# Two seven-product groups in the first strip pair of each chunk of the second MLP's down-projection

## What is computed

```python
def causal_dwconv(u, conv_w, conv_b):
    ...
    for t in range(CONV_WIDTH):
        out = out + up[:, t:t + S] * conv_w[t]
...
        h = rms_norm_2(x, pre_ffn_g[l])
        up = causal_dwconv(h @ w_up[l], conv_w[l], conv_b[l])
        y = (jax.nn.gelu(up[..., :D_FF_2], approximate=True) * up[..., D_FF_2:]) @ w_down[l]
        x = x + rms_norm_2(y, post_ffn_g[l])
```

## Time and profile before

| | us |
|---|---|
| device time, median of 3 runs (2079.47 to 2080.83) | 2079.84 |
| the profiled execution's own time | 2080.22 |
| its span, first to last instruction | 2078.4 |
| TensorE busy | 2067.9 (99%) |
| VectorE busy | 1413.8 (68%) |
| ScalarE busy | 1136.4 (55%) |

### The profile page before, as it was taken

How to read it: one execution, slowest core, us unless ns; L and a number is a source line. 1 busy time by engine, 2 the same in 40 slices (tenths; PEclk the granted TensorE clock), 3 DMA queues, 4 the chain that set the end, 5 groups by cost and what they waited for, 6 DMA issues and landing times.

```text
span 2078.4 us, 24128 instructions
## 1 busy us (share of the span) xinstructions
PE 2067.9 (99%) x9229; PEld 1714.6 (82%) x9229; DVE 1413.8 (68%) x1618; ACT 1136.4 (55%) x1384; POOL 60.1 (3%) x55
## 2 busy tenths in 40 slices
PE   9999999999999999999999999999999999999998
PEld 7888888888888888888888888888888888888887
DVE  6446556777886779777876655566767775576665
ACT  7555655555554555555655544455555544555553
POOL 3000000000000000000002000000000000000010
PEclk9999999999999999999999999999999999999999
DMA  8687666778666776678678787677787757778763
GB/s 294 194 262 228 190 186 217 245 242 254 216 199 200 242 239 201 213 237 269 223 258 238 218 250 231 192 212 223 243 253 233 234 181 214 237 228 262 244 212 122
DMA packets 291907, 469.50 MB, mean 226 GB/s; under 512 B 18512, under 2 KB 82128, under 8 KB 291280
## 3 DMA queue, kind: packets, MB, share of 16 engines
q1 hardware_dynamic: 290928, 463.46, 71.5%
q10 hardware_dynamic: 864, 4.49, 0.6%
HBM read 432.75 MB, written 35.13 MB: 225 GB/s over the span
## 4 chain that ended last, share of the span: by engine, by line
PE 96%; DMA 2%; DVE 1%; ACT 1%; issue 0%; SPq 0%; ACTq 0%; DVEq 0%
PE ps L1842 96%; DMA passed_rows<-xN 1%; DVE Wl L1428 1%; DMA E<-passed_rows 0%; ACT Wh L1192 0%; DMA raw<-in_sb_w_qkv_dram 0%; DVE xN L1577 0%; DVE T L1587 0%; PE ps L1845 0%; SPq L1105 0%; ACT aHL L1214 0%; ACT T L1208 0%; DVE hid L1616 0%; DVE aHL L1591 0%; SPq L1100 0%
## 5 line engine op out<-in xcount | busy, mean ns | idle before, releaser
L1428 DVE TENSOR_TENSOR Wl<-raw,Wh 128x1024 fp32r<-128x1024 f32 x743 | 908.1, 1241 | 534.5 <-ACT Wh L1192 527.4
L1842 PE MATMUL ps<-Wh,aHL 128*128 128x512 f32 x3642 | 1129.2, 390 | 2.6 <-DVE aHL L1591 0.9
L1192 ACT ACTIVATE Wh<-raw 128x1024 fp32r<-128x1024 f32 x743 | 771.0, 1055 | 517.2 <-PE ps L1842 492.8
L1842 PEld LDWEIGHTS ps<-Wh,aHL 128*128 128x128 f32 x3642 | 684.0, 188 | 146.5 <-issue 1.7
L1842 PE MATMUL ps<-Wl,aHL 128*128 128x512 f32 x1821 | 708.7, 389 | 0.0
L1842 PE MATMUL ps<-Wh,hid 128*128 128x512 f32 x1548 | 480.2, 389 | 0.0
L1842 PEld LDWEIGHTS ps<-Wl,aHL 128*128 128x128 f32 x1821 | 342.1, 188 | 70.2
L1842 PEld LDWEIGHTS ps<-Wh,hid 128*128 128x128 f32 x1548 | 290.6, 188 | 60.5 <-DVE xN L1577 0.2
L1842 PE MATMUL ps<-Wl,hid 128*128 128x512 f32 x774 | 301.1, 389 | 0.0
L1842 PEld LDWEIGHTS ps<-Wl,hid 128*128 128x128 f32 x774 | 145.3, 188 | 30.0
L1842 PE MATMUL ps<-Wh,oHL 128*128 128x512 f32 x512 | 158.8, 390 | 0.0
(11 more groups left out here) (218 smaller groups left out, 1003.8 us busy)
## 6 DMA issues: line engine op xcount, KB each, us to landing
raw<-in_mlp_w_dram SPq DMA_DIRECT2D x256, 512.0 KB, 4.9
raw<-in_w_up_dram SPq DMA_DIRECT2D x176, 512.0 KB, 4.4
raw<-in_sb_w_qkv_dram SPq DMA_DIRECT2D x93, 512.0 KB, 5.1
raw<-in_w_down_dram SPq DMA_DIRECT2D x88, 512.0 KB, 4.7
raw<-in_w_in_dram SPq DMA_DIRECT2D x64, 512.0 KB, 5.2
passed_strip<-T SPq DMA_DIRECT2D x88, 256.0 KB, 4.4
T<-passed_strip SPq DMA_DIRECT2D x176, 128.0 KB, 4.5
raw<-in_sb_w_o_dram SPq DMA_DIRECT2D x32, 512.0 KB, 5.4
```

The costliest lines, as they stand in the source:

```text
L1192: e.activation(Wh[:, i % NW, c], src, ACT.Copy).then_inc(st["hi"][0], 1)
L1428: e.tensor_tensor(Wl[:, i % NW, c], src, Wh[:, i % NW, c].bitcast(F32), ALU.subtract).then_inc(st["lo"][0], 1)
L1842: return e.matmul(o, l, r, start=start, stop=stop, skip_group_check=True)
```

## The change

In the first strip pair of each chunk, the first two row pieces of both strips (`sevens=(2 * at, 2 * at + 1)`) become two groups. `lead` is new: 2n - 4 plain pieces of the first strip (8 in chunk 0, 6 in chunk 1), all but its tail, stand ahead of the first group; three pieces of the second strip stand between the groups, five (chunk 0) or three (chunk 1) behind the second, then the tails. Chunk 1 now makes mixed tokens for its first strip. In chunk 1 the fold adds to rows that exist (eight VectorE operations), and the steps `y_sum` wait for it. The diff, cut to its core:

```diff
@@ def strip_pair
-    def strip_pair(w, s4, ks, tail, mov, tiles, evacs, koff=0, sevens=(), fold=None):
+    def strip_pair(w, s4, ks, tail, mov, tiles, evacs, koff=0, sevens=(), fold=None, lead=None):
...
-        lead, gap = (4, 3) if tail else (2, 3 if len(plain) > 7 else 2)
+        lead, gap = (lead or 4, 3) if tail else (2, 3 if len(plain) > 7 else 2)
@@ def evac_conv
-    def evac_conv(j, which, t0, last, at_first):
+    def evac_conv(j, which, t0, last):
...
-                    if at_first and t0 in MIXED_STRIPS:
+                    if t0 in MIXED_STRIPS and (j < 6 or t0 == 0):
                         free["E"] = [lo, mix_tokens("hid2", "E", *MIXED_STRIPS[t0], [g])]
@@ def evac_y
-                kw = dict(t=t, s4=s4, set=s, mm=k[t], t0_free=list(free["T0"]), y=y, q=q, g=g, g_row=st["g_row"])
+                kw = dict(t=t, s4=s4, set=s, mm=k[t], t0_free=list(free["T0"]), y=y, q=q, g=g, g_row=st["g_row"],
+                          folded=st.get(("fold", s4)))
@@ the loop over the two chunks
             i = strip_pair("w_down_2", s4, tuple(range(2 * at, 2 * (at + n))), 0 if s4 else 2, "hid2", hid_tiles,
                            [evac_y(c, s4), evac_y(c, s4 + 1)], koff=2 * at,
-                           sevens=(2 * at, 2 * at + 1, 2 * at + 4) if c == 0 and s4 else (),
-                           fold=fold_into("xn", s4, fresh=True))
+                           sevens=(2 * at, 2 * at + 1, 2 * at + 4) if c == 0 and s4 else (2 * at, 2 * at + 1) if s4 == 0 else (),
+                           fold=fold_into("xn", s4, fresh=c == 0), lead=None if s4 else 2 * n - 4)
@@ vector_program, the steps y_sum and y_last
                     e.wait_ge(*st["mm"])
+                    if st["folded"]:
+                        e.wait_ge(*st["folded"])
                     e.tensor_tensor(xn[:, t, cs], xn[:, t, cs], ps[st["set"]][:, t, :], ALU.add).then_inc(st["y"][0], 1)
```

More of the change, by code:

```diff
@@ L798, in plan_program @@
             for which in range(2):
-                i = strip("w_up_2", which * 5632 + (at + j) * STRIP, ALL8, "aHL", tile_hl, evac_conv(at + j, which, 4 * j, j == n - 1, c == 0))
+                i = strip("w_up_2", which * 5632 + (at + j) * STRIP, ALL8, "aHL", tile_hl, evac_conv(at + j, which, 4 * j, j == n - 1))
                 if at + j + which == 0:
```

## The result

The changed kernel takes **2085.95 us** (median of 9 runs, 2082.85 to 2087.44) where the kernel before takes 2080.62 beside it (2079.47 to 2083.07): 1.0025 times as long, with an interval of 1.0016 to 1.0033. The forecast was 2081.9 with a range to 2084.0, so the time lies outside, on the slow side.

The account below looks back on a forecast made before the run. TensorE, busy 99%, was taken as the bound, so only removed matmuls could gain. Two pairs, each 2.28 + 0.10 - 1.36 = 1.02 us lost, add 2.0 to the median 2079.84: forecast 2081.9 us, range 2078.2 to 2084.0.

Parts of the forecast that it names:

- The matmuls: Two groups in each of two pairs remove 12 matmuls of 0.227 us: 2.72 us saved, 1.36 per pair.
- The wait: At the first plain piece behind either pair's second group, TensorE waits 2.28 us on `Wl`; bounds 1.1 to 3.4.
- X: The moment TensorE ends s1 (second split buffer) of the first group, releasing the split of a later plain piece.
- The chain: ScalarE's and VectorE's queued work from X until TensorE can start the plain piece behind the second group: 17.24 us.
- The other side of the sum: TensorE's work from X until the plain piece behind the second group is due: 66 matmuls, 14.96 us.
- the released split: ScalarE's split, starting at X, of the third plain piece between the groups; 1.09 us until VectorE's low half starts.
- the slow first matmul: The first matmul after a wait takes 0.33 us instead of 0.227, so 0.10 us was added per wait.
- What costs nothing: Mixed tokens, loads and later `y_sum` cost nothing; chunk 1's fold just fits, 9.38 us against 9.44.
- the rival that the clock falls in the gaps: Behind the new waits the clock drops to 1.2 GHz, one piece at either place, giving 2087.3 us; chance 0.05.
- the sum said 2.0: Both pairs together lose 2.0 us: per pair 2.28 + 0.10 - 1.36 = 1.02.
- The row leaned on: The stretch behind the 2.26 us gap shows a granted clock of 1.00, taken as no drop near that length.
- The gap leaned on: TensorE's 2.26 us gap before the last two matmuls, about the longest in the trace, compared with the expected 2.2 us.

Follow-up runs that it names:

- orders without a wait: Changed kernel with all plain pieces of the second strip between the groups (2077.88 against 2080.28; again 2078.15 against 2080.92), or five (2077.74 against 2080.92).
- the first series: The changed kernel's first timing against the kernel before: 2085.95 us against 2080.62, ratio 1.0025.
- the second series: The changed kernel timed once more, unaltered, against the kernel before: 2084.46 us against 2080.78, ratio 1.0018.

## Why the prediction was right and wrong

**The matmuls.** Right: 12 fewer, worth 2.7 us. The orders without a wait show it (2.4, 2.8 and 3.2 us below before), and in their profiles a pair is 1.33 to 1.36 us shorter.

**The wait.** Right in place and cause, and 0.27 us too small at either place. ScalarE's and VectorE's timelines of the changed kernel, chunk 1, from X on (the moment from which the prediction followed the queues; ScalarE starts there at 1986.36, in chunk 0 at 1642.73):

```profile
1986.36 1.06 ACT L1193 ACTIVATE Wh<-raw 128x1024 fp32r<-128x1024 f32 x1 [0.30 <-PE ps L1845]
...
1994.67 2.08 ACT L1349 ACTIVATE E<-T,conv 128x256 f32<-128x256 f32 x4 [2.49 <-DVE T L1552]
1996.66 0.62 ACT L1193 ACTIVATE Wh<-wsum 128x512 fp32r<-128x512 f32 x1
```

```profile
1988.60 0.68 DVE L1435 TENSOR_TENSOR wsum<-raw 128x512 f32<-128x512 f32 x1
...
1993.40 1.24 DVE L1552 STREAM_TRANSPOSE T<-T 128x1024 f32<-128x1024 f32 x1
...
1997.31 0.69 DVE L1429 TENSOR_TENSOR Wl<-wsum,Wh 128x512 fp32r<-128x512 f32 x1 [1.56 <-ACT Wh L1193]
1997.92 3.24 DVE L1708 SCALAR_TENSOR_TENSOR E<-T,conv,E 128x255 f32<-128x255 f32 x8
2001.19 1.23 DVE L1714 TENSOR_TENSOR E<-E,zs 128x1024 f32<-128x1024 f32 x1
2002.34 4.62 DVE L1429 TENSOR_TENSOR Wl<-raw,Wh 128x1024 fp32r<-128x1024 f32 x4
```

Term by term, measured against forecast: split and low half to 1988.60, 2.24 (2.23); sums and two low halves to 1993.40, 4.80 (4.81); turning to 1994.67, 1.27 (1.27); newest tap to 1996.66, 1.99 (1.97); split of s3 to 1997.31, 0.65 (0.66); its low half 0.61 (0.61); taps 3.27 (3.27); gate 1.15 (1.14); last low half to TensorE's start at 2003.61, 1.27 (1.28). The chain is 17.25 us where 17.24 was forecast, and 17.26 in chunk 0 (1642.73 to 1659.99). The other side of the sum was 0.26 too long: 14.96 us from 1986.36 make the next piece due at 2001.32, but it was due at 2000.83 + 0.23 = 2001.06, since TensorE starts s2 that much before ScalarE starts the released split. So TensorE loses 2.55 us, forecast 2.28, and the slow first matmul is 0.33 as the earlier trace rows have it. From its first matmul to the first behind it, chunk 1's pair took 54.40 us before and takes 55.74, 1.3 more, and chunk 0's 65.28 and 68.23, 2.95 more with its fall.

**What costs nothing.** Right: no wait from the mixed tokens, the loads or the first pairs' folds, in the changed kernel or the orders without its wait. With four pieces between the groups a load did cost, 1.25 us in chunk 1.

**The clock.** Here the prediction failed. Of the rival that the clock falls in the gaps it said: "Chance 0.05, because the one row near that length shows no drop", and it left the rival out of the sum and the range. A fall took place in nearly every run: in 18 of the 20 timed runs of the changed kernel the mean clock is 0.998 or less. With no fall the forecast nearly holds: the two runs at 0.999 took 2082.8, 2.0 to 2.2 above before, and the sum said 2.0. What lies above that is falls, about two in the median run of the first series (5.3 - 2.1 = 3.2, mean clock 0.997) and one in the second (3.7 - 2.1 = 1.6, mean clock 0.998). Some are those behind the wait near 400 us, which the kernel before has too: 6 of 26 timed runs in the second series stand at 0.998, 2.1 us or more above the median of the rest (the place is inferred, for the one profile of that kernel has no fall there). Of the 4.05 us by which the forecast was low, 0.8 is the kernel before, which took 2080.62 beside the changed one and not 2079.84, 0.5 the two waits, and the rest, 2.7, the falls.

Three things made the chance too small. The row leaned on, 2073:2074 with 1.00, ends 0.8 us after the restart at 2073.22, and there are no more matmuls to see. In the changed kernel the clock was still 1.00 a microsecond after the restart and fell then. And one execution was read as a rule, where equal waits of one execution go both ways. The gap leaned on shows this itself. It is 2.25 to 2.26 us in all 13 profiles, at a place that no kernel here changes. The two matmuls behind it take 1.12 to 1.17 us together in eight of them, the kernel before among them, and 1.51 to 2.08 in five, where the clock goes to 0.50; so with one group in each pair:

```profile
2072.14 2.07 PE L1845 MATMUL ps<-QK,zs 128*128 128x512 f32 x2 [2.26 <-ACT zs L1373]
...
2073.00:2074.00 1.00, 1.00 (x2) 0.00 (x0) 0.76 (x2) 0.00 (x0) 0.00 (x0) 0.50 0.72 268
```

## What to carry to other kernels

Before putting work on VectorE or ScalarE, write down from the buffer that releases the next split what both queues still hold, in order, against the matmuls that TensorE has until then. Short pieces shrink that cover; move them away from other long work (here two plain pieces more between the groups turned 3.7 to 5.3 us lost into 3.2 gained). Count a new wait of TensorE of 2 to 3 us as its length and, in about half of the cases here, 1.6 us for the clock, and look at the granted clock well past a restart (the falls here lay within 6 us of it), in more than one execution.

## What was not expected of the hardware

Whether the clock falls is not settled by the length of the wait alone. All profiles here together, ahead of the last normalisation: after waits of up to 1.66 us none; after 1.81 a fall; after 1.86 none; after 2.28 a fall; after 2.34 none; after 2.38 to 2.39 four falls in six; after 2.98 none and after 2.99 a fall; after 3.54 two in two. The gap of 2.25 to 2.26 us in the last normalisation adds five falls in 13, as far as the two matmuls behind it can tell. In two profiles of the changed kernel equal waits of one execution, in chunk 0 and chunk 1, went different ways. What decides at a given length stays open; no kernel was made to vary it. Two of the list by their rows, a fall behind 2.28 us near 400 us, with five pieces between the groups, and none behind 2.98 with four:

```profile
399.67 0.47 PE L1845 MATMUL ps<-Wh,aHL 128*128 128x512 f32 x1 [2.28 <-DVE aHL L1592]
...
401.00:403.00 2.00, 2.00 (x6) 1.58 (x5) 1.63 (x5) 1.74 (x3) 0.00 (x0) 0.50 0.00 0
```

```profile
400.76 0.47 PE L1845 MATMUL ps<-Wh,aHL 128*128 128x512 f32 x1 [2.98 <-DVE aHL L1592]
...
401.00:403.00 2.00, 2.00 (x10) 1.61 (x10) 1.54 (x3) 1.98 (x2) 0.00 (x0) 1.00 0.24 92
```

The wait near 400 us itself, for rows that go out and back by DMA, came out between 0.95 and 2.99 us in thirteen profiles of kernels that do not differ there.
